# Squares of the keys on ScalarE, key factor and root in one product, scan operands in PSUM, and the falling exponentials in two halves

## What is computed

```python
def rwkv7_time_mix(pb, w0, w_lora_up, a0, a_lora_up, g_lora_up, k_k, k_a, r_k, lnx_g, lnx_b):
    ...
    w = -jax.nn.softplus(-(w0 + jnp.tanh(xw) @ w_lora_up).astype(f32)) - 0.5
    decay = jnp.exp(-jnp.exp(w))
    a = jax.nn.sigmoid((a0 + xa @ a_lora_up).astype(f32))
    g = (jax.nn.sigmoid(xg) @ g_lora_up).astype(f32)
    ...
    kk = k * k_k.astype(f32).reshape(B_HEADS, B_HEAD_DIM)
    kk = kk / jnp.maximum(jnp.sqrt(jnp.sum(kk * kk, axis=-1, keepdims=True)), 1e-12)
    k = k * (1.0 + (a - 1.0) * k_a.astype(f32).reshape(B_HEADS, B_HEAD_DIM))
    ...
    bonus = (jnp.sum(r * k * r_k.astype(f32), axis=-1, keepdims=True) * v).reshape(bsz, seq, B_WIDTH)
    return ((o + bonus) * g).astype(pb.dtype)
```

## Time and profile before

| | us |
|---|---|
| plain runs, median of 3 | 1082.75 (1082.58 to 1083.18) |
| profiled execution, device time | 1088.29 |
| profiled execution, span from first to last instruction | 1086.5 |
| TensorE busy in the span | 1069.7 |
| VectorE busy | 710.4 |
| ScalarE busy | 612.8 |
| GpSimd busy | 476.5 |

### The profile page before, as it was taken

One profiled execution on the slowest core, in us unless ns is written; L12 is line 12 of the kernel. 1 busy time (PEld: TensorE's weight loads), 2 busy tenths in 40 slices (PEclk: granted clock), 3 DMA queues, 4 the chain that ended last, 5 costly groups with the idle time before them and its releaser, 6 DMA issues.

```text
span 1086.5 us, 23067 instructions
## 1 busy us (share of the span) xinstructions
PE 1069.7 (98%) x7680; PEld 993.2 (91%) x7680; DVE 710.4 (65%) x1479; ACT 612.8 (56%) x1118; POOL 476.5 (44%) x224
## 2 busy tenths in 40 slices
PE   8979999999999999999999999999999999999997
PEld 7879899999999999999999999998888888888886
DVE  7792873434629999145888888884555555555554
ACT  6653355465555445455777777774445454444444
POOL 4656723487317888888777777760000000000000
PEclk9989999999999999999999999999999999999999
DMA  7443402255644555555444444445556555565553
GB/s 262 139 165 125 136 21 78 78 177 191 215 155 156 180 187 174 186 179 176 157 154 157 155 155 155 158 165 175 193 193 193 193 193 193 193 193 193 193 193 135
DMA packets 52131, 181.21 MB, mean 167 GB/s; under 512 B 5811, under 2 KB 7859, under 8 KB 51964
## 3 DMA queue, kind: packets, MB, share of 16 engines
q1 hardware_dynamic: 51660, 180.13, 50.2%
q10 hardware_dynamic: 432, 0.55, 0.1%
HBM read 179.60 MB, written 1.06 MB: 166 GB/s over the span
## 4 chain that ended last, share of the span: by engine, by line
PE 84%; issue 5%; POOL 5%; DVE 3%; ACT 1%; DMA 0%; POOLq 0%; ACTq 0%; DVEq 0%
PE PS L412 14%; PE PS L413 13%; PE PS L414 13%; PE PS L809 11%; PE PS L811 11%; PE PS L810 11%; POOL lo L1206 5%; PE PS L760 1%; PE PS L761 1%; PE PS L599 1%; PE PS L607 1%; PE PS L555 1%; PE PS L586 1%; DVE arena L1363 0%; DMA xT<-in_x_t 0%
## 5 line engine op out<-in xcount | busy, mean ns | idle before, releaser
L1206 POOL TENSOR_TENSOR lo<-raw,hi 128x1024 fp32r<-128x1024 f32 x191 | 465.7, 2443 | 219.2 <-ACT hi L860 207.3
L860 ACT CAST hi<-raw 128x1024 fp32r<-128x1024 f32 x331 | 346.4, 1047 | 206.3 <-DMA raw<-in_v_units 170.8
L412 PE MATMUL PS<-xh,hi 128*128 128x256 f32 x1352 | 391.6, 290 | 6.0 <-ACT hi L860 5.7
L413 PE MATMUL PS<-xl,hi 128*128 128x256 f32 x1352 | 383.9, 284 | 0.0
L414 PE MATMUL PS<-xh,lo 128*128 128x256 f32 x1352 | 383.6, 284 | 0.0
L1254 DVE TENSOR_TENSOR lo<-raw,hi 128x1024 fp32r<-128x1024 f32 x140 | 171.7, 1226 | 157.4 <-ACT hi L860 157.4
L412 PEld LDWEIGHTS PS<-xh,hi 128*128 128x128 f32 x1352 | 260.1, 192 | 9.0 <-issue 7.4
L413 PEld LDWEIGHTS PS<-xl,hi 128*128 128x128 f32 x1352 | 260.2, 192 | 0.1
L414 PEld LDWEIGHTS PS<-xh,lo 128*128 128x128 f32 x1352 | 260.1, 192 | 0.0
L809 PE MATMUL PS<-hi,xh 128*128 128x512 f32 x512 | 199.7, 390 | 0.3 <-issue 0.3
L811 PE MATMUL PS<-lo,xh 128*128 128x512 f32 x512 | 199.4, 390 | 0.0
(11 more groups left out here) (291 smaller groups left out, 1167.0 us busy)
## 6 DMA issues: line engine op xcount, KB each, us to landing
raw<-in_u_units SPq DMA_DIRECT2D x128, 512.0 KB, 3.3
raw<-in_v_units SPq DMA_DIRECT2D x128, 512.0 KB, 3.3
raw<-in_w_in_units SPq DMA_DIRECT2D x43, 512.0 KB, 3.4
raw<-in_w_q_units SPq DMA_DIRECT2D x16, 512.0 KB, 3.4
raw<-in_w_proj_units SPq DMA_DIRECT2D x8, 512.0 KB, 3.3
raw<-in_w_out_units SPq DMA_DIRECT2D x8, 512.0 KB, 3.3
arena<-bias_rows SPq DMA_DIRECT2D x2, 512.0 KB, 5.0
arena<-in_subkeys_t SPq DMA_DIRECT2D x1, 1024.0 KB, 5.7
```

The source lines that it names most:

```text
L412: mm(ps, hi[:, s, c], mh[:, k, :], start=(k == k0), stop=False)
L413: mm(ps, hi[:, s, c], ml[:, k, :], start=False, stop=False)
L860: nc.scalar.copy(hi[:, j, :], raw[:, j, :]).then_inc(hi_made, 1)
L1206: nc.gpsimd.tensor_tensor(lo[:, w, :], raw[:, w, :], hi[:, w, :].bitcast(F32), ALU.subtract).then_inc(lo_pool, 1)
```

## The change

ScalarE squares the keys: right after the cast of unit 7, which is moved ahead, it loads the sigmoid table and makes tmp = (kB x factor) squared in four instructions that each count `kk_sq`; the head sums wait for four. The cast of unit 8 goes between the two halves of the sigmoids. VectorE no longer makes kk from the factor ahead of the roots, nor the square, nor the scaled block constants; kk is made in four instructions from kB, the factor and the inverse root, and rk in four that take the factor r_k in, so that the bonus sums use the plain block constant. `scan_ones` and `mids` move to PSUM bank 3: the ones are written there once the first two sigmoids have emptied it, the scans run before `mix_in(5, 6)`, and `mids` is a copy of five columns a channel tile. Unit 10, which writes bank 3, waits for `mid_made`. `mix_in` 7, 8 and 9 move between the steps of the root. The falling exponentials run four before and four after `gate_copy(14)`, which casts unit 16.

```diff
-        scan_ones = area(R0 + 11268, T)
+        scan_ones, mids = PS[:, 3, T:2 * T], PS[:, 3, 0:20].rearrange("p (c n) -> p c n", n=5)
-        blk_rk = area(R0 + 15872, 512, CT, P)
...
+                if g == GATE_AT[0]:
+                    pe.wait_ge(mid_made, 1)
...
-            pe.wait_ge(kk_sq, 1)
+            pe.wait_ge(kk_sq, CT)
...
-            pe.wait_ge(blk_made, 1)
             for c in range(CT):
-                last = mm(PS[:, 4 + c // 2, T * (c % 2):T * (c % 2) + T], blk_rk[:, c, :], rk[:, c, :], start=True, stop=True)
+                last = mm(PS[:, 4 + c // 2, T * (c % 2):T * (c % 2) + T], blk, rk[:, c, :], start=True, stop=True)
...
-                    if g not in (MIX_AT[10], 12):
+                    if g not in (5, 6, MIX_AT[10], 12):
...
             mix_evac(3, 4)
+            hi_ahead(5, 0, 0)
+            nc.scalar.preload_act_table(ACT.Sigmoid)
+            act.wait_ge(mix_made, 5)
+            for c in range(CT):
+                nc.scalar.activation(tmp[:, c, :], kB[:, c, :], ACT.Square, scale=vec[:, V_KK + c:V_KK + c + 1]
+                                     ).then_inc(kk_sq, 1)
...
+                if c2 == 0:
+                    hi_ahead(6, 0, 0)
...
+            falling(0, 1)
             gate_copy(14)
+            falling(2, 3)
...
-            V.memset(scan_ones, 1.0)
...
-            dve.wait_ge(mix_made, 5)
-            for c in range(CT):
-                last = V.tensor_scalar(kk[:, c, :], kB[:, c, :], per_channel(V_KK + c), None, ALU.mult)
-            link(last)
-            V.tensor_tensor(tmp, kk, kk, ALU.mult).then_inc(kk_sq, 1)
-            dve.wait_ge(const_in, 16)
-            for c in range(CT):
-                last = V.tensor_scalar(blk_rk[:, c, :], blk, per_channel(V_RK + c), None, ALU.mult)
-            last.then_inc(blk_made, 1)
-            mix_in(5, 6)
+            dve.wait_ge(lor_sb, 2)
+            link(V.memset(scan_ones, 1.0))
...
             scan(0, 1)
-            mix_in(7)
             link(scan(2, 3))
-            mids = Lz[:, :, HD:HD + P + 1:P]
...
+            mix_in(5, 6)
+            link(V.tensor_copy(mids, Lz[:, :, 0:T + 1:HD]))
+            V.tensor_tensor(fall_0, mids[:, :, 1:4:2], Lz[:, :, 0:P + 1:P], ALU.subtract)
...
+            mix_in(7)
             link(V.reciprocal(roots[:, 0:2, :], roots[:, 0:2, :]))
+            mix_in(8)
+            link(V.reciprocal(roots[:, 2:4, :], roots[:, 2:4, :]))
+            dve.wait_ge(mix_made, 5)
+            for c in range(CT):
+                last = V.scalar_tensor_tensor(out=kk[:, c, :], in0=kB[:, c, :], scalar=per_channel(V_KK + c),
+                                              in1=roots[:, c, :], op0=ALU.mult, op1=ALU.mult)
+            last.then_inc(kk_made, 1)
             mix_in(9)
-            link(V.reciprocal(roots[:, 2:4, :], roots[:, 2:4, :]))
-            V.tensor_tensor(kk, roots, kk, ALU.mult).then_inc(kk_made, 1)
...
-            V.tensor_tensor(rk, rB, k2, ALU.mult).then_inc(rkv_made, 1)
+            for c in range(CT):
+                last = V.scalar_tensor_tensor(out=rk[:, c, :], in0=rB[:, c, :], scalar=per_channel(V_RK + c),
+                                              in1=k2[:, c, :], op0=ALU.mult, op1=ALU.mult)
+            last.then_inc(rkv_made, 1)
```

More of the change, by code:

```diff
@@ L288, in block_program @@
                                                   sem("st_sb"))
-        o_ps, var_ps, ob_made, blk_made = sem("o_ps"), sem("var_ps"), sem("ob_made"), sem("scaled_blocks_made")
+        o_ps, var_ps, ob_made = sem("o_ps"), sem("var_ps"), sem("ob_made")
         y_made, h_made = sem("y_made"), sem("h_made")
@@ L981, in _, with falling @@
             mix_evac(11)
-            act.wait_ge(kk_made, 1)
-            for c in range(CT):
-                for n in range(NT):
-                    m = 32 + 2 * c + n
-                    nc.scalar.activation(fall[:, c, n, :], Lz[:, c, P * n + 1:P * n + P + 1], ACT.Exp,
-                                         bias=small[:, m:m + 1], scale=-decay).then_inc(e_made, 1)
+            def falling(*cs):
+                for c in cs:
+                    for n in range(NT):
+                        m = 32 + 2 * c + n
+                        nc.scalar.activation(fall[:, c, n, :], Lz[:, c, P * n + 1:P * n + P + 1], ACT.Exp,
+                                             bias=small[:, m:m + 1], scale=-decay).then_inc(e_made, 1)
+            act.wait_ge(kk_made, 1)
+            falling(0, 1)
             gate_copy(14)
+            falling(2, 3)
             mix_evac(12, 13)
@@ L1367, in _ @@
             scan(0, 1)
-            mix_in(7)
             link(scan(2, 3))
-            mids = Lz[:, :, HD:HD + P + 1:P]
-            V.tensor_tensor(fall_0, mids, Lz[:, :, 0:P + 1:P], ALU.subtract)
-            V.tensor_scalar(small[:, 32:40].rearrange("p (c n) -> p c n", n=2), mids, decay, None, ALU.mult)
-            V.tensor_scalar(small[:, 40:48].rearrange("p (c n) -> p c n", n=2), mids, -decay, None, ALU.mult)
-            V.tensor_tensor(small[:, 52:56].unsqueeze(2), mids[:, :, 0:1], mids[:, :, 1:2], ALU.subtract
+            mix_in(5, 6)
+            link(V.tensor_copy(mids, Lz[:, :, 0:T + 1:HD]))
+            V.tensor_tensor(fall_0, mids[:, :, 1:4:2], Lz[:, :, 0:P + 1:P], ALU.subtract)
+            V.tensor_scalar(small[:, 32:40].rearrange("p (c n) -> p c n", n=2), mids[:, :, 1:4:2], decay, None, ALU.mult)
+            V.tensor_scalar(small[:, 40:48].rearrange("p (c n) -> p c n", n=2), mids[:, :, 1:4:2], -decay, None, ALU.mult)
+            V.tensor_tensor(small[:, 52:56].unsqueeze(2), mids[:, :, 1:2], Lz[:, :, HD + P:HD + P + 1], ALU.subtract
                             ).then_inc(mid_made, 1)
@@ L1379, in _ @@
             link(last)
-            mix_in(8)
             roots = PS[:, KK_BANKS[0]:KK_BANKS[1] + 1, :].rearrange("p b (c t) -> p (b c) t", c=2)
```

## The result

| | kernel before | changed kernel |
|---|---|---|
| six plain runs, median | 1084.03 us | 1078.56 us |
| lowest and highest | 1082.58, 1087.41 | 1078.06, 1079.93 |
| profiled execution, device time | 1088.29 | 1078.70 |
| profiled execution, span | 1086.5 | 1076.9 |
| ratio of times | | 0.9945 (0.9926 to 0.9964) |

The six runs of the kernel before are the three shown ahead of the prediction and three more, 1084.88, 1086.89 and 1087.41; its profiled execution is none of them. The profiled execution of the changed kernel is the first of its six.

What follows compares the result with a forecast made beforehand. Bound: TensorE waiting for unit 16's late cast, the lower clock behind it, and the head sums' wait. 1.17 + 5.95 + 2.61 = 9.73 us, less 0.7, gives 9.0; 1082.75 - 9.0 = 1073.7 us, range 1072.0 to 1077.0.

Steps and rivals of the forecast that it cites:

- The step that failed: Profiled 1088.29 against plain median 1082.75: stage taken to cost the same in both, 9.0 us taken off the median.
- A second reading: TensorE's 2.06 us gap before the head sums: claimed not to lower the clock, unlike the 5.72 us gap.
- The aside: Unit 16: if plain runs do not fall to the lower clock there, 2.6 us less saved, 1076.3, within the range.
- A: Head sums: squares on ScalarE, start at 35.46 instead of 36.63, 1.17 us gained (0.65 to 1.4), 0.9 gap left.
- B: VectorE's scans with ones in PSUM: 0.63 to 0.66 us each, mid_made near 37.6, unit 10 not delayed, cost nothing.
- C: Key factor on VectorE: kk_made near 51 instead of 68.0, so ScalarE's 5.34 us wait before the falling exponentials goes.
- D: Falling exponentials in halves around unit 16's cast: 5.95 us idle time and 2.61 us of lower clock saved.
- E: GpSimd's subtractions for units 14 to 16 delayed by VectorE's rk and aB products: 0.7 us lost (0 to 2.7).
- R1: GpSimd becomes late: three subtractions late by 1.1 us more, 3.3 us lost, 1077.0 us; chance 0.13.
- R2: kk_made and unit 16's cast stay late, only the head-sum gain left: 1081.5 us; chance 0.06, shared with losses behind L534.
- R3: GpSimd sets the pace of units 11 to 21, 4.0 us a unit against 2.88: 1085.3 us; chance 0.03.
- R4: No loss at GpSimd's subtractions and the head-sum gap wholly gone: 10.6 us saved, 1072.1; chance 0.78 together with the forecast.

Runs made afterwards that it cites:

- before_sixth: The kernel before, unchanged, profiled once more: 1082.61 us.
- eight_first: The changed kernel with all eight falling exponentials ahead of gate_copy(14), as before: 1080.18 us, ratio 0.9945 to the kernel before.
- before_again: The kernel before, unchanged, profiled again: 1087.84 us; twelve runs 1082.80 to 1088.41.
- before_fifth: The kernel before, unchanged, profiled again in the third group: 1087.26 us.
- seven_first: The changed kernel with unit 7 ahead of the head sums on TensorE: 1077.35 us, ratio 0.9921 to the kernel before.
- seven_again: The changed kernel with unit 7 ahead of the head sums, run again beside the changed kernel on one chip: 1077.53 us, ratio 0.9934.
- psum_only: The kernel before with only the ones and middles moved to PSUM bank 3, unit 10 waiting for mid_made: 1082.35 us, ratio 0.9973.
- after_again: The changed kernel, unchanged, run again in the first group: 1079.00 us, ratio 0.9929; profiled at 1079.07.
- after_third: The changed kernel, unchanged, run again in the fourth group: 1078.74 us, ratio 0.9945 to the kernel before.
- rk_one: The changed kernel with rk in one product instead of four, the factor r_k left out: 1079.54 us, ratio 0.9942 to the kernel before.
- before_third: The kernel before, unchanged, profiled a third time: 1085.1 us.
- before_fourth: The kernel before, unchanged, profiled a fourth time: 1084.13 us.
- tensor_extra: The kernel before with three useless matmuls more ahead of the head sums: 1083.61 us, ratio 0.9987.
- before_seven: The kernel before with unit 7 ahead of the head sums: 1088.31 us, ratio 1.0016.
- falling_late: The kernel before with the eight falling exponentials behind the gate copy of unit 14, so behind the cast of unit 16: 1082.95 us, ratio 0.9976.
- gap_longer: The changed kernel with three more squares on ScalarE, so that the head sums wait longer: 1081.27 us.

## Why the prediction was wrong in its number and, in the main, right in its steps

**The step that failed** is "I take the stage to cost the same in both and take the saving off the median". The three plain runs and the profiled execution differed by 5.5 us, and I took that for an offset of the profiler. The changed kernel shows no such offset: 1078.70 profiled, 1078.56 the median. The 5.5 us was the stage itself: kk_made came 4.4 us later (68.0 against 63.6), nearly all of it by two blocked small instructions, and behind that stood a gap of 5.7 us in front of unit 16 and the lower clock after it, all of which short runs don't have. Taken off the profiled time, the same saving of 9.0 us would have given 1088.3 - 9.0 = 1079.3, within 0.8 us of the result. A second reading failed with it, that "the gap of 2.06 us at L509 had no such effect": in the long course it had none, in the short one the clock fell behind it and cost 1.6 us. The only row that stood ahead and speaks of it is the time of 1088.29 beside three runs within 0.6 us of each other.

**What a short run saves.** The starts of ScalarE's copies, read from the timelines of the three profiles, tell it unit by unit:

| copy of unit | before, long | before_sixth | changed | before_sixth less changed |
|---|---|---|---|---|
| 9 | 50.71 | 52.24 | 49.50 | 2.74 |
| 13 | 62.22 | 63.76 | 61.02 | 2.74 |
| 15 | 72.54 (late on ScalarE itself) | 70.28 | 66.94 | 3.34 |
| 16 | 79.44 | 73.64 | 69.82 | 3.82 |
| 17 | 82.51 | 76.99 | 72.70 | 4.29 |
| 21 | 94.03 | 88.50 | 84.22 | 4.28 |

2.74 us up to unit 13 are the earlier head sums (36.55 to 35.43, 1.12) and the lower clock behind them (the other 1.6). In the 1.55 from there to unit 17 the units run late by some 0.5 us each behind the eight exponentials in a block; eight_first puts the block alone at 1.2. Together 4.3, against a fall of 4.2 from 1082.75 to 1078.56. On the long course it is 9.8 (94.03 to 84.22), 9.6 in the span. That is the dearest of three long profiles: from the head sums to the copy of unit 21 before_again took 56.29 us and before_fifth 56.19, the one ahead of the prediction 57.40.

**The aside** "if the plain runs do not fall to the lower clock there, 2.6 us less is saved, 1076.3" saw the place and not the size: they had neither the lower clock there nor the 5.7 us wait.

**A, head sums**: right within its bounds. The start is 1.20 us earlier for 1.17, but the fifth mix copy already stood 0.20 earlier (27.01 and 27.21), which is luck; the gap shrank by 1.00, from 2.06 to 1.06, where 0.9 was to be left. Squares took 0.43 us each for 0.35; seven_first and seven_again price the gap left at 1.1 to 1.2.

**B, the scan**: right. 1.27 us a pair, mid_made at 37.2 for 37.6, no wait of TensorE in front of unit 10.

**C, the key factor**: right. kk_made at 50.5 for 51; the four joined products took 1.66 us. No run shows what C earns by itself: psum_only is without it and has no wait for kk_made either, and neither has the short course.

**D, the halves**: right, on the long course. From unit 13 to unit 21 the saving grew from 1.20 to 9.81, by 8.6 us; D less E was forecast at 8.56 - 0.7 = 7.9.

**E, what is late next**: within its bounds, dearer than measured by 0.1 to 0.5 us. Against three units of 2.88 the copies of units 13 to 16 are late by 0.16 us in the first profile of the changed kernel, 0.50 in after_again and 0.59 in after_third; 0.7 was forecast. I had GpSimd wait for rk. In the first profile it was the other way round: rk stood behind two of GpSimd's subtractions and took 6.05 us, and nobody was waiting for it. In the other two rk stood behind one and took 3.83 and 3.84, and the subtraction of unit 14 took 2.56 and 2.55 us for 2.40, so each waited for the other once. The single product of rk_one holds GpSimd longer (2.89) than the four do. The Trainium skill, SBUF — State Buffer, "Who interferes with whom", says that the one that issues later is blocked; that alone did not tell which one would be later, and here it changed from run to run.

**The rivals.** R1 (GpSimd late) was not there, though its 1077.0 comes near the result by chance: three late subtractions were to cost 3.3 us, and the units that E speaks of are late by 0.2 to 0.6 together. R2 and R3 fell with kk_made at 50.5 and TensorE busy throughout. R4 was near on E in one profile of three and wrong about A's gap.

**Open.** Why the clock fell behind the gap of 2.06 us in three profiles of the kernel before and not in the other three, and in seven of twelve runs behind 2.25, no run settles; nor why it cost 1.1 to 1.2 us less behind the gap of 5.7 to 5.9 us in before_again and before_fifth than in the profile ahead of the prediction. The runs between 1084 and 1086.6 are explained in part: before_third (1085.1) began its head sums 1.1 us later still than the others, and before_fourth (1084.13) has one more wait of 1.0 us, for VectorE's L1321. The head sums of the kernel before start anywhere from 36.48 to 37.75 in its six profiles behind the same gap, so up to 1.3 us of scatter comes from ahead of this stage. For the runs without a trace, the course is inferred from their time and mean clock.

## What to carry to other kernels

Before a saving is subtracted, see whether the profiled execution and the plain runs are the same course: if they lie further apart than the plain runs among themselves, subtract from the profiled time and name two cases for the plain one. A kernel whose engines meet by a hair's breadth, here a difference of eight elements that starts 0.6 us behind the start of a subtraction (50.05 and 49.45) or 1.0 us ahead of it (49.95 and 50.98), can take either side in each run, and then a small delay can speed it up (tensor_extra) and a removed wait can bind it to the worse side (before_seven). Most of what this change gains on the long course is that its chain no longer meets the subtractions where somebody waits for it, and its runs lie within 1.9 us instead of 6 to 7.

## What the runs showed of the hardware that was not expected

- A gap of TensorE of 2.06 us was followed by a lower granted clock in three of nine profiles (six of the kernel before, one each of falling_late, psum_only and tensor_extra), one of 1.06 us in none of five. In the three, and in gap_longer, it cost 1.5 to 1.7 us between the start of the head sums and the copy of unit 9 (15.62 to 15.75 us for 14.08).
- Gaps of 5.7 to 6.5 us were followed by the lower clock in all four profiles that have one, but not for the same time: from 74 to 80 the mean clock was 0.52 in the profile ahead of the prediction and 0.77 in before_fifth, both behind 5.7 us.
- The length of a VectorE instruction says little of what blocking costs it: eight elements a partition stood 2.2 us (0.18 free), a 128x1024 product 3.29 (1.22), four products of 128x256 6.05 in two blocks and 3.83 in one, k2 with one SBUF operand 3.28 in one and 5.25 in two (1.13 free).
- Scans with one operand in PSUM took 1.26 to 1.27 us a pair wherever they were looked at, beside subtractions too (psum_only); with both in SBUF, 4.90 to 4.92 there.
